# HGRN heads pipelined one iteration deeper: a head's score levels in the iteration after its projections, projections in the order v, f, q

## What is computed

```python
    proj = h @ w_in
    q, f, i, g = jnp.split(proj, 4, axis=-1)
    k = (1.0 - lb) * jax.nn.sigmoid(-ff)
    qf = jax.nn.silu(q.astype(jnp.float32)) * (HGRN_HEAD_DIM ** -0.5)
    ...
    """S_t = diag(f_t) S_{t-1} + k_t v_t^T ; o_t = S_t^T q_t.  All (B,S,H,X) float32."""
    ...
    o = o * lax.rsqrt(jnp.mean(o * o, axis=-1, keepdims=True) + NORM_EPS)
    o = o.reshape(b, s, D_MODEL) * out_norm.astype(jnp.float32) * jax.nn.silu(g.astype(jnp.float32))
    return o.astype(h.dtype) @ w_out
```

## Time and profile before

| | |
|---|---|
| runs shown | 2515.36, 2514.09, 2518.74 us; median 2515.36 |
| profiled execution, span from first to last instruction | 2511.6 us |
| its own time | not given apart; the median is 3.8 us above the span |
| PE busy | 2444.9 us (97%), 11520 instructions |
| PEld busy | 2038.0 us (81%) |
| DVE busy | 1118.2 us (45%) |
| ACT busy | 417.4 us (17%) |
| POOL busy | 742.1 us (30%) |
| mean granted clock of PE | 0.992 |

### The profile page before, as it was taken

How to read it: one execution, slowest core, us unless ns; L and a number is a source line. 1 busy time by engine, 2 the same in 40 slices (tenths; PEclk the granted TensorE clock), 3 DMA queues, 4 the chain that set the end, 5 groups by cost and what they waited for, 6 DMA issues and landing times.

```text
span 2511.6 us, 29616 instructions
## 1 busy us (share of the span) xinstructions
PE 2444.9 (97%) x11520; PEld 2038.0 (81%) x11520; DVE 1118.2 (45%) x1449; ACT 417.4 (17%) x691; POOL 742.1 (30%) x420
## 2 busy tenths in 40 slices
PE   7999999899999999999999999999999999999998
PEld 5778888788888888888888888888888888888886
DVE  7777777865321221221366666555421131221233
ACT  4222222212210210200231002002220120110210
POOL 2121111233333333333332222333233333332331
PEclk9999999999999999999999999999999999999999
DMA  3101010022111111111111111111111111111112
GB/s 134 34 27 33 25 33 25 26 100 67 42 50 50 50 44 49 50 50 46 46 50 67 34 42 43 42 42 51 42 50 45 48 50 50 48 44 50 50 50 75
DMA packets 36639, 123.05 MB, mean 49 GB/s; under 512 B 4704, under 2 KB 4832, under 8 KB 36576
## 3 DMA queue, kind: packets, MB, share of 16 engines
q1 hardware_dynamic: 35568, 120.54, 15.0%
q10 hardware_dynamic: 1008, 1.62, 0.2%
HBM read 117.95 MB, written 4.19 MB: 49 GB/s over the span
## 4 chain that ended last, share of the span: by engine, by line
PE 90%; DVE 6%; DVEq 2%; issue 1%; ACT 1%; DMA 0%; SPq 0%; ACTq 0%
PE prod_ps L377 27%; PE prod_ps L379 27%; PE prod_ps L378 27%; DVE hgrn_qk L888 2%; PE side_ps L507 2%; PE side_ps L423 2%; PE side_ps L429 1%; DVEq L895 1%; PE side_ps L437 1%; PE side_ps L447 1%; PE side_ps L439 1%; DVE sq_sum L791 1%; DVE x_res L1140 1%; DVE hgrn_scores L914 0%; PE side_ps L456 0%
## 5 line engine op out<-in xcount | busy, mean ns | idle before, releaser
L377 PE MATMUL prod_ps<-operand_hi,w_hi 128*128 128x512 f32 x3264 | 1289.6, 395 | 12.3 <-DVE operand_lo L795 11.8
L379 PE MATMUL prod_ps<-operand_hi,w_lo 128*128 128x512 f32 x3264 | 1276.1, 391 | 0.0
L378 PE MATMUL prod_ps<-operand_lo,w_hi 128*128 128x512 f32 x3264 | 1275.5, 391 | 0.0
L377 PEld LDWEIGHTS prod_ps<-operand_hi,w_hi 128*128 128x128 f32 x3264 | 616.5, 189 | 139.6 <-POOL w_lo L325 8.9
L379 PEld LDWEIGHTS prod_ps<-operand_hi,w_lo 128*128 128x128 f32 x3264 | 615.5, 189 | 130.3
L378 PEld LDWEIGHTS prod_ps<-operand_lo,w_hi 128*128 128x128 f32 x3264 | 616.5, 189 | 123.9
L323 POOL CAST w_hi<-w_raw 128x1024 fp32r<-128x1024 f32 x200 | 208.0, 1040 | 1688.3 <-PE prod_ps L379 1682.9
L325 POOL TENSOR_TENSOR w_lo<-w_raw,w_hi 128x1024 fp32r<-128x1024 f32 x200 | 516.2, 2581 | 16.0
L1092 DVE SCALAR_TENSOR_TENSOR work<-prod_ps,inv_rms 128x512 f32<-128x512 f32 x128 | 88.4, 692 | 493.3 <-PE prod_ps L379 492.7
L1104 DVE TENSOR_TENSOR x_res<-prod_ps,x_res 128x512 f32<-128x512 f32 x96 | 66.4, 691 | 432.9 <-PE prod_ps L379 432.9
L1510 ACT ACTIVATE work<-work 128x512 f32<-128x512 f32 x128 | 81.0, 633 | 1044.9 <-DVE work L1092 1044.9
(11 more groups left out here) (151 smaller groups left out, 1194.6 us busy)
## 6 DMA issues: line engine op xcount, KB each, us to landing
w_raw<-stream SPq DMA_DIRECT2D x204, 512.0 KB, 3.5
x_in<-x_t SPq DMA_DIRECT2D x16, 256.0 KB, 6.6
x_res<-x_t SPq DMA_DIRECT2D x8, 512.0 KB, 4.4
out_t<-x_res SPq DMA_DIRECT2D x16, 256.0 KB, 2.1
masks_f<-masks SPq DMA_DIRECT2D x1, 896.0 KB, 9.0
ret_rows<-head_rows ACTq DMA_DIRECT2D x1, 512.0 KB, 3.5
ret_cos<-rope ACTq DMA_DIRECT2D x1, 512.0 KB, 4.4
ret_sin<-rope ACTq DMA_DIRECT2D x1, 512.0 KB, 5.2
```

The lines of the kernel that those rows point to most:

```text
L377: nc.tensor.matmul(prod_ps[:, bank], w_h, a_h, start=(k == 0), stop=False)
L378: nc.tensor.matmul(prod_ps[:, bank], w_h, a_l, start=False, stop=False)
L379: last = nc.tensor.matmul(prod_ps[:, bank], w_l, a_h, start=False, stop=(k == KT - 1))
```

## The change

The levels of a head are now done in the iteration after its projections, levels 0 to 6, and level 7 and the rest in the iteration after that. Iteration n of PE: product 1 with (v, level 7 of head n-2) in its middle and level 0 of head n-1 behind it; product 2 with k of head n-2, level 1 of head n-1 behind; product 3 with kv and level 2, T behind; product 4 with level 3, then o and level 4; product 5 whole, then level 5; product 6 with back and level 6. There is one more iteration, 9, whose products are gate units 3 to 5. Projections come as v, f, q, so iteration n takes v first. Scores and v have two buffers; v lies with them in other rooms. The count of taken steps is kept for each pair of PSUM banks, and a step waits only until its own pair is free, and for the data it reads. `heads_done` comes after iteration 9. SP's and POOL's code is the same as before.

The order and the tiles:

```diff
-HG_ORDER = ("L3", "L4", "L5", "L6", "L7", "v", "k", "back", "kv", "T", "o", "L0", "L1", "L2")
-HG_OPEN = {0: ("L0", "L1", "L2"), 1: tuple(x for x in HG_ORDER if x != "back"),
-           HEADS1: tuple(x for x in HG_ORDER if x not in ("L0", "L1", "L2"))}
+HG_ORDER = ("v", "L7", "L0", "k", "L1", "kv", "L2", "T", "L3", "o", "L4", "L5", "back", "L6")
+HG_NEWER = ("L0", "L1", "L2", "L3", "L4", "L5", "L6")
+HG_OLDER = tuple(x for x in HG_ORDER if x not in HG_NEWER)
...
-T_HGRN2 = T_HGRN + len(HG_OPEN[0]) + len(HG_OPEN[1])
-T_HGRN_END = T_HGRN2 + len(HG_ORDER) * (HEADS1 - 2) + len(HG_OPEN[HEADS1])
-T_NORM1 = T_HGRN_END + 1
+T_HGRN2 = T_HGRN + len(HG_NEWER)
+T_HGRN_LAST = T_HGRN2 + len(HG_ORDER) * (HEADS1 - 1)
+T_NORM1 = T_HGRN_LAST + len(HG_OLDER)
...
-        h_qk = [place(f"hgrn_qk{b}", [P, 2, S], at=a + b * 16 * KB) for b in range(2)]
-        h_q, h_k = [t[:, 0] for t in h_qk], [t[:, 1] for t in h_qk]
-        h_s = place("hgrn_scores", [P, NB, BLK], at=a + 24 * KB)
+        h_v_t = [place(f"hgrn_v_t{b}", [P, S], at=a + b * 28 * KB) for b in range(2)]
+        h_kq = [place(f"hgrn_kq{b}", [P, 2, S], at=a + 4 * KB + b * 12 * KB) for b in range(2)]
+        h_k, h_q = [t[:, 0] for t in h_kq], [t[:, 1] for t in h_kq]
+        h_s = [place(f"hgrn_scores{b}", [P, NB, BLK], at=a + 12 * KB + b * 12 * KB) for b in range(2)]
...
-        h_v_t = place("hgrn_v_t", [P, S], at=a + 8 * KB)
...
-        side_taken = sem("side_taken")
+        side_taken = [sem("side_taken_even"), sem("side_taken_odd")]
```

The waits on PE:

```diff
-            def all_taken(t):
-                if not (isinstance(t, int) and t < 1):
-                    pe.wait_ge(side_taken, t)
-            def one_back(t):
-                if not (isinstance(t, int) and t < 2):
-                    pe.wait_ge(side_taken, t - 1)
+            def pair_free(step):
+                if not (isinstance(step, int) and step < 2):
+                    pe.wait_ge(side_taken[step_pair(step)], earlier_uses(step))
+                return step_pair(step)
+            def taken_from(step):
+                pe.wait_ge(side_taken[step_pair(step)], earlier_uses(step, 2))
+            def all_taken(step):
+                if not (isinstance(step, int) and step < 1):
+                    pe.wait_ge(side_taken[1 - step_pair(step)], earlier_uses(step, 1))
+                return pair_free(step)
```

PE's steps (removed functions left out):

```diff
+                def newer_level(number):
+                    if newer:
+                        level(number, n - 1, prev)
+                def turn_v_and_last_level():
...
+                        pair = pair_free(hgrn_step(n, "v"))
+                        pe.wait_ge(evac, n * 6 - 10)
+                        turn(pair, h_v_t[par])
+                        level(LEVELS - 1, n - 2, par)
+                def turn_k():
+                    if older:
+                        pe.wait_ge(level_fed, n * LEVELS - LEVELS)
+                        turn(pair_free(hgrn_step(n, "k")), h_k[par])
+                def chunk_kv():
+                    if older:
+                        taken_from(hgrn_step(n, "v"))
+                        taken_from(hgrn_step(n, "k"))
+                        blocks_128(pair_free(hgrn_step(n, "kv")), lambda c: h_k_t[:, c], lambda c: h_v[:, c], NB - 1)
+                def turn_scores():
+                    if older:
+                        taken_from(hgrn_step(n, "L7"))
+                        turn(pair_free(hgrn_step(n, "T")), h_s[par][:].rearrange("p c t -> p (c t)"),
+                             range(1, NB, 2))
+                def out():
+                    if older:
+                        pe.wait_ge(states_ready, n - 1)
+                        taken_from(hgrn_step(n, "T"))
+                        outputs(pair_free(hgrn_step(n, "o")), h_v, h_s[par], h_state, h_q[par])
+                def back():
+                    if older:
                         pe.wait_ge(o_normed, n - 1)
...
+                        turn(pair_free(hgrn_step(n, "back")), o_keep)
+                def kv_then_second_level():
+                    chunk_kv()
+                    newer_level(2)
+                def out_then_fourth_level():
+                    out()
+                    newer_level(4)
+                def back_then_sixth_level():
+                    back()
+                    newer_level(6)
                 u = n * 3
                 slots = [(u + j // 2, (par + j // 2) % 2, j % 2) for j in range(6)]
-                mids = [older_levels(3), older_levels(5), level7_and_v, chunk_kv, out, newer_levels(1)]
-                ends = [older_levels(4), older_levels(6), turn_k_and_back, turn_scores, after_fifth, newer_levels(2)]
+                mids = [turn_v_and_last_level, turn_k, kv_then_second_level, lambda: newer_level(3), None,
+                        back_then_sixth_level]
+                ends = [lambda: newer_level(0), lambda: newer_level(1), turn_scores, out_then_fourth_level,
+                        lambda: newer_level(5), None]
                 for j, (uu, slot, half) in enumerate(slots):
                     if mid_start and j < 4:
                         continue
                     product(uu, slot, half, 0, mid=mids[j])
-                    ends[j]()
```

DVE's order:

```diff
+                        h = 3 * (n - HEADS1) + j // 2
+                        gate_mul(ho, G_OUT1, h, j % 2, 2 * h + j % 2 + 1)
+                    elif j >= 4:
+                        dve.wait_ge(q_sig, n * 2 + (j - 3))
+                        q = h_q[par][:, tokens(j - 4)]
+                        last = nc.vector.scalar_tensor_tensor(q, q, float(P) ** -0.5, sig[:, j - 4],
+                                                              ALU.mult, ALU.mult)
+                        if j == 5:
+                            last.then_inc(qk_ready, 1)
+                            dve.drain()
...
-                older_level(3)
+                        h = 3 * (n - HEADS1) + j // 2
+                        gate_low(h, j % 2, 16 + 2 * h + j % 2 + 1)
+                if older:
+                    copied(h_v[:].rearrange("p c v -> p (c v)"), "v")
+                    level(par, LEVELS - 1)
+                newer_level(0)
                 group(0)
-                older_level(4)
                 if older:
-                    norm_factor(n - 1)
+                    copied(h_k_t[:].rearrange("p c k -> p (c k)"), "k")
+                newer_level(1)
                 second(0)
-                older_level(5)
                 group(1)
                 third(0)
-                older_level(6)
                 if older:
-                    normed(n)
-                second(1)
-                older_level(7)
-                if attend:
-                    nc.vector.tensor_copy(h_v[:].rearrange("p c v -> p (c v)"), take("v")).then_inc(side_taken, 1)
-                group(2)
-                third(1)
-                if attend:
-                    nc.vector.tensor_copy(h_k_t[:].rearrange("p c k -> p (c k)"), take("k")
-                                          ).then_inc(side_taken, 1)
-                if older:
-                    o_at = ho[:, n - 2] if static else ho[:, bass.ds(n - 2, 1)].rearrange("p a s -> p (a s)")
-                    nc.vector.tensor_copy(o_at, take("back")).then_inc(side_taken, 1)
-                second(2)
-                if attend:
-                    kv = take("kv").rearrange("p (c v) -> p c v", c=NB)
+                    step = hgrn_step(n, "kv")
+                    kv = done_step(step).rearrange("p (c v) -> p c v", c=NB)
...
-                    last.then_inc(side_taken, 1)
+                    last.then_inc(taken(step), 1)
                     dve.drain()
                     dve.sem_inc(states_ready, 1)
+                newer_level(2)
+                if older:
+                    step = hgrn_step(n, "T")
+                    turned = done_step(step).rearrange("p (c t) -> p c t", c=NB)
+                    nc.vector.tensor_copy(h_s[par][:, 1::2], turned[:, 1::2]).then_inc(taken(step), 1)
+                second(1)
+                group(2)
+                third(1)
+                newer_level(3)
+                if older:
+                    copied(o_keep[:], "o")
+                    dve.drain()
+                    dve.sem_inc(o_kept, 1)
+                newer_level(4)
+                second(2)
                 group(3)
-                if attend:
-                    turned = take("T").rearrange("p (c t) -> p c t", c=NB)
-                    nc.vector.tensor_copy(h_s[:, 1::2], turned[:, 1::2]).then_inc(side_taken, 1)
                 third(2)
+                if older:
+                    norm_factor(n - 1)
+                newer_level(5)
                 second(3)
+                group(4)
+                third(3)
                 if project:
                     dve.wait_ge(gates, n * 2 + 2)
                     at = slice(n, n + 1) if static else bass.ds(n, 1)
                     nc.vector.tensor_scalar(h_d[0][:], h_d[0][:], lb[:, 4, at], lb[:, 3, at], ALU.mult, ALU.add)
```

(54 more changed lines are left out.)

297 lines of the change are left out of this document (132 added, 165 removed).

## The result

Both kernels ran on the same chip, one after the other. The changed kernel takes **2535.43 us** (median of 4 runs, 2534.29 to 2536.75), the kernel before 2514.73 there (2512.52 to 2518.74): a ratio of 1.008, with a 95% interval of 1.0068 to 1.0093. The profiled execution after took 2536.75 us; its span is 2534.8 us against 2511.6, so 23.2 longer. The forecast was 2543.5, in a range of 2525 to 2556: the direction and the range hold, and the point is 8.1 us too high. The medians are 20.7 us apart, less than the profiled spans, since the profiled execution after is the slowest of its four.

What follows compares the result with a forecast made beforehand. PE bounds the kernel, busy 2444.9 of 2511.6 us. From 2515.4: +6.0 iterations 2 to 7, -3.8 start, +9.2 iterations 8 and 9, +12.0 gate unit 6, +4.7 clock = +28.1, so 2543.5 us; eight-in-ten range 2525 to 2556.

Steps and rivals of the forecast that it cites:

- New wait 1: At back, iterations 2 to 8: PE waits 3.1 us each time for `normed`, queued on DVE behind level 5, take and gates.
- New wait 2: At level 2, iterations 1 to 8: PE waits 1.6 us (3.0 in iteration 1) for level 1's copies, held by POOL's split.
- Rival (b): At level 1: DVE's second multiply wins the port from POOL, so level 2 does not wait; 2530 us, chance 0.11.
- Small new wait: At level 7, early in the iteration: its gather on ACT is 0.2 us late, an estimate between 0 and 0.5.
- Switches: On PE, each iteration: two of twelve switches between products and steps go, at some 0.12 us each, -0.25 us.
- the term of **6.0: Iterations 2 to 7: new waits less the 3.7 us removed and 0.25 for fewer switches, +1.0 each, six times, +6.0 us.
- The sign that an iteration would take 54.5 to 56.5 us: In the profile after, one iteration of the HGRN stage takes 54.5 to 56.5 us; before, 53.78 or 55.35.
- Iterations 8 and 9: End of the heads: DVE late with levels and gates, idle 11.3 and 6.0 us, together 17.3 in place of 7.7; +9.2 us.
- Gate unit 6: PE waits for unit 6's load and split, since the load now follows `heads_done` after iteration 9; +12.0 us.
- Clock: PE's clock: six falls in the stage where there were four, and one more behind the 12 us wait; +4.7 us.
- The base: Start of the sum: profiled span 2511.6 us, median of the runs 3.8 above it, untouched by the change; 2515.4 us.
- Rival (a): HGRN stage: the levels' waits vanish and no new one comes, though unit 6 still costs 12.0 + 1.6; 2490 us, chance 0.07.

Runs made afterwards that it cites:

- Experiment 5: Against the changed kernel: `normed` ahead of level 5 on DVE, its root earlier on ACT, gate units 6 and 7 loaded before SP waits for `heads_done`; 2491.11 us.

## Why the prediction was right

The mechanism held in its three main steps, and it is they that give the sign. The prediction said what the chain on DVE would do to back, what the meeting on the port would do to level 2, and what the signal would do to unit 6, and the experiments take each away by itself: 30 us for the first (with its share of the clock), 15 for the third, 9 for the second once the other two are mended. The sizes, in the prediction's terms:

- **New wait 1.** Forecast 3.1 us, measured 2.88 twice and 2.95 to 2.97 four times in iterations 2 to 7. PE reaches back 3.82 us after level 5's start (forecast 3.7), and `normed` ends after 6.64 (forecast 6.75).
- **New wait 2.** Forecast 1.6, measured 1.43 in each of seven iterations; in iteration 1 forecast 3.0, measured 1.73, since there the two levels do not share a pair of banks and only the gather is late. Rival (b), that DVE wins the port, did not come true: in all eight meetings POOL's subtraction began 0.38 to 0.39 us ahead of the second multiply.
- **Small new wait.** Forecast 0.2 for level 7's gather, not there in iterations 2 to 8.
- **Switches.** Forecast -0.25 an iteration, measured -0.40 (50.05 less 49.65). With the three above an undisturbed iteration grew by 0.25 us (53.78 to 54.03) and not by 1.0. So the term of **6.0** was 1.5. The sign that an iteration would take 54.5 to 56.5 us held for neither end: 54.03 to 56.77.
- **Iterations 8 and 9.** Forecast 17.3 us of idle time. Measured 1.43 for level 2, 2.0 for T, 4.57 for back, 3.8 for level 7 and 1.72 for the last back: 13.6. The 2.3 for level 4 in iteration 8, where a set of gates was to be late, is not there, nor the 0.5 for T in iteration 9. This is the step that was read wrong: DVE was taken as late at a point where it was not. (The terms named for iteration 8 add up to 11.1; the 11.3 comes out with the small new wait of 0.2.)
- **Gate unit 6.** Forecast +12.0, measured 11.97. The load landed by 545.90, 4.05 us after its issue at 541.85, and not after 3.5; the signal came 4.4 us after PE's end (4.5), and the split took 3.5 instead of 3.8. The Trainium skill ("DMA: Bandwidth & Descriptors", on the anatomy of one DMA), from which the prediction estimated 3.2 us for the load and 11.7 for the wait, lies farther from this load than the row.
- **Clock.** Forecast +4.7. It was nearly twice that. The idle terms of the forecast are 61.7 us from iteration 1 to unit 6 and the measured ones 53.5, so 8.2 too many; the busy time was to grow by 2.8 and grew by 6.1, although the switches gave back 1 to 1.5 us more than forecast. By this the clock cost 8.5 to 9.5; half of the time that PE works at a granted 0.5, summed over both traces, gives 8.5 as well (an estimate, 15.0 against 6.5). The forecast counted six falls of one length where there had been four, and one behind unit 6. The trace has seven ahead of unit 6: in iterations 2, 4, 6 and 7, each at the wait of back, and three in iterations 8 and 9. So the count was nearly right and the length was not: the fall of iteration 6 cost PE 2.7 us (52.39 against 49.65) and that of iteration 4 1.5 (51.17), and the one behind unit 6 about 2.2.
- **The base.** The forecast took the runs to lie 3.8 us above the profiled span. The profiled run after lies 1.95 us above its own span, so 1.9 of the 8.1 us are this. Another 1.3 are the profiled run's distance from the median, and 4.9 the sum itself (28.1 against 23.2).

So two errors stood against each other: waits 8.2 us too long, and the work of PE 3.3 us too short (the clock too cheap by 4 to 5 us, the switches by 1 to 1.5). The nearness of the sum (23.2 measured, 28.1 forecast) is partly this, and so partly luck. One reading at the start was loose too: the profile's chain gives PE 90% and the products' three lines 81%, so "nine tenths" holds for PE as a whole. What the forecast did get from the rows is the sign and its three causes.

Rival (a), 2490 us, gave as its deciding point that `normed` ends within 3.7 us of level 5's start. Experiment 5 puts `normed` there and also mends unit 6: 2491.1. That the two numbers agree is mostly chance, since (a) still had the loss at unit 6, and in its place no wait of level 2.

## What to carry to other kernels

When a pipeline is made deeper, its new waits come from the engines whose order was carried over: list for each step what must be done before it and what is queued ahead of that, on every engine. Here one VectorE operation that ran 4.5 us after its data were there, and one load that hung on a signal at the end of the heads, turned a gain of 0.9% into a loss of 0.8%. Where two engines hold each other up, one of the two operations can be moved to where its neighbours don't mind; when the whole group of splits was moved, the next operation was held. And read from the code in what units a semaphore counts before a shift is put in microseconds: here "half a product, 3 us" was a whole one, 8.9 us.
